# State-space parameters made in the first projection, the scan spread between the steps of a sparse attention written out over all heads

## What is computed

```python
proj = h @ w_in                       # h: normed x
u, q, k, v, qi, ki, wi, gates = split(proj)
# state-space branch, 32 groups of 16 channels, 64 complex states each
abar = exp(ar * dt) * (cos(ai * dt) + i sin(ai * dt))
coef = (abar - 1) / (ar + i ai)
s_t = abar * s_(t-1) + coef * (B @ u_t)
y = gelu(real(C @ s) + D_skip * u)
y = y * sigmoid(y @ w_glu + b_glu)
# sparse attention, 8 heads of 64, one shared key head: of the visible keys
# the 256 with the best index score take part
o = softmax(q k^T / 8 over the chosen keys) @ v
merged = sigmoid(g_ssm) * (y @ w_proj_ssm) + sigmoid(g_att) * (o @ w_proj_attn)
```

## Time and profile before

| | us |
|---|---|
| median of 3 runs | 4801.21 (4798.48 to 4808.43) |
| profiled execution | 4806.75 |
| its span in the profile | 4805.1 |

### The profile page before, as it was taken

The page is one execution under the profiler, slowest core; times in us unless marked ns, Lnnn a source line. Parts: engine busy times, 40 slices in busy tenths (PEclk is TensorE's granted clock), DMA queues, the critical chain, the costliest instruction groups (busy, mean ns, idle before and its releaser), DMA issues. The chain is left out here.

```text
span 4805.1 us, 54891 instructions
## 1 busy us (share of the span) xinstructions
PE 4013.4 (84%) x20836; PEld 3406.9 (71%) x20836; DVE 2033.1 (42%) x3688; ACT 1524.9 (32%) x2712; POOL 1522.1 (32%) x1187
## 2 busy tenths in 40 slices
PE   8598741568999989999999674666999999999878
PEld 6467641447888878788888553555879888988867
DVE  2289436332200013353111255875346666566623
ACT  2144531011200013321111233554334555545433
POOL 1121102013332324211111253322445555555433
PEclk9789875589999999998999776877999999999989
DMA  3122110035312144422221233332521111111044
GB/s 114 55 69 76 41 31 9 12 138 198 131 59 79 42 148 156 128 94 99 101 85 64 71 98 88 78 81 81 176 78 36 45 44 36 45 45 42 22 153 140
DMA packets 279840, 395.28 MB, mean 82 GB/s; under 512 B 56075, under 2 KB 183212, under 8 KB 279596
## 3 DMA queue, kind: packets, MB, share of 16 engines
q1 hardware_dynamic: 249452, 290.08, 20.0%
q0 software_dynamic: 27856, 97.88, 5.4%
q10 hardware_dynamic: 2304, 4.20, 0.2%
HBM read 285.72 MB, written 101.01 MB: 80 GB/s over the span
## 5 line engine op out<-in xcount | busy, mean ns | idle before, releaser
L112 PE MATMUL out_acc<-out_sw,out_sa 128*128 128x512 f32 x1920 | 447.0, 396 | 50.3 <-POOL out_sa L606 43.0
L112 PEld LDWEIGHTS out_acc<-out_sw,out_sa 128*128 128x128 f32 x1920 | 367.0, 191 | 130.3 <-issue 44.3
L112 PE MATMUL hg_acc<-l_XT,hg_ws 128*128 128x512 f32 x1440 | 360.3, 408 | 0.0
L112 PE MATMUL hg_acc<-l_first_ws,l_XT 128*128 128x256 f32 x2880 | 359.6, 284 | 0.0
L112 PEld LDWEIGHTS hg_acc<-l_first_ws,l_XT 128*128 128x128 f32 x2880 | 348.8, 192 | 0.0
L112 PEld LDWEIGHTS hg_acc<-l_XT,hg_ws 128*128 128x128 f32 x1440 | 278.5, 197 | 57.8
L3238 POOL TENSOR_TENSOR hg_DD<-hg_BB 128x256 f32<-128x256 f32 x224 | 157.1, 701 | 355.3 <-PE hg_pA L3002 228.8
L112 PE MATMUL up_acc<-ffn_XT,ffn_first_ws 128*128 128x512 f32 x1152 | 263.6, 391 | 2.7 <-PEq L52 2.7
L112 PE MATMUL down_acc<-down_sw,down_sa 128*128 128x512 f32 x1056 | 241.9, 391 | 19.1 <-POOL down_sa L606 16.7
L606 POOL TENSOR_TENSOR out_sa<-out_a,out_sa 128x512 fp32r<-128x512 f32 x80 | 175.8, 2198 | 253.1 <-ACT out_sw L505 253.0
L112 PEld LDWEIGHTS up_acc<-ffn_XT,ffn_first_ws 128*128 128x128 f32 x1152 | 217.3, 189 | 48.0 <-issue 2.9
(11 more groups left out here) (489 smaller groups left out, 8219.3 us busy)
## 6 DMA issues: line engine op xcount, KB each, us to landing
l_first_raw<-in_odd_w_in SPq DMA_DIRECT2D x62, 512.0 KB, 5.4
down_w<-in_w_ffn_down SPq DMA_DIRECT2D x44, 512.0 KB, 3.8
da_raw<-q_k SPq DMA_DIRECT2D x32, 512.0 KB, 8.3
out_w<-in_even_w_out SPq DMA_DIRECT2D x32, 512.0 KB, 4.3
out_w<-in_odd_w_out SPq DMA_DIRECT2D x32, 512.0 KB, 4.3
even_w<-in_even_w_in SPq DMA_DIRECT2D x7, 2048.0 KB, 9.2
l_first_raw<-in_even_w_in SPq DMA_DIRECT2D x6, 2048.0 KB, 9.1
hidden<-up_h POOLq DMA_DIRECT2D x44, 256.0 KB, 2.3
```

Of the source, the lines that this page charges most:

```text
L112: mm = pe.matmul(out, lhs(p, k), rhs(q, k), start=start and i == 0, stop=stop and i == n - 1)
```

## The change

**Parameters.** A new class `StateSpace` holds the parameters' buffers. Its eight loads are issued by SP at the end of `input_norm`, behind the first weights. `first_projection` takes the place of `project`: its weights have one raw buffer in place of two, SP in place of POOL issues the stores, DVE does the parameters between the splits, POOL makes `Wn`, and behind the last product TensorE transposes `Wn` and makes the kernels through the same banks, evictions and stage buffers. E, CP, the transposed input weights and the kernels go to memory (`kept`).

**Attention and scan.** `attend_and_scan` takes the place of `sparse_attend` and `s5_branch`. It has no loop: all 64 items are written out and numbered through, and the queries of the next pair are rounded at the middle of a pair. Logits have three buffers instead of four; `pO` is one bank instead of two, and the bank set free is `acc`, the only one of the scan branch. The table `place` says at which item and spot each of 40 groups of four (transposed inputs, input sums, output sums, transposed outputs, mixing) stands. The scan is cut in two halves of 1024 elements and 32 steps, one behind each item from 11 on. `CP` takes the buffer of E, and `MT` that of the input weights, when the scan has ended.

The diff, cut to its core:

```diff
 # input_norm, SP
                 pre.load(sp, pre_ld)
+                ss.load(sp)
 # first_projection, SP
+                load(1)
+                for i in range(N + TURNS + KERNELS):
+                    b = i % B
+                    sp.wait_ge(moved, i + 1)
...
+                    if i == G - 2:
+                        sp.wait_ge(e_made, 1)
+                        sp.dma_start(kept["E"], ss.wide[:, 0:S_E]).then_inc(e_st, DMA)
+                        sp.dma_start(kept["m8"], at["m8"]).then_inc(e_st, DMA)
+                    if i % G == G - 1 and i // G + 2 < len(chunks):
+                        load(i // G + 2)
+                    if i == N - 1:
+                        sp.wait_ge(cp_made, 1)
+                        sp.dma_start(kept["CP"], ss.wide[:, :]).then_inc(cp_st, DMA)
 # DVE
+                dve.wait_ge(ss.loaded, ss.loads * DMA)
+                expm1_of("e", "ldt", 5)
...
+                dve.wait_ge(phase, 2)
...
+                dve.sem_inc(e_made, 1)
+                split_weights(1)
...
+                dve.sem_inc(powers, 1)
+                dve.wait_ge(e_st, 2 * DMA)
+                for k in range(S_T + 1):
+                    if k == 1:
+                        split_weights(2)
+                    ss.cmul(dve, link, (CP[:, 0, :, k, :], CP[:, 1, :, k, :]), (ss.Cn[:, 0, :, :], ss.Cn[:, 1, :, :]),
+                            [wide_of(q) for q in pw(k)], shape, neg=True)
 # ACT, behind the eviction of group 1
+                    if i == 1:
+                        act.wait_ge(phase_in, 1)
+                        act.activation(at["sn"], at["r"], ACT.Sin).then_inc(phase, 1)
+                        act.activation(at["cs"], at["h"], ACT.Sin).then_inc(phase, 1)
 # attend_and_scan
+    for k in range(8):
+        place[2 + k // 2, k % 2] = TURN_U + k
+        place[6 + k // 2, k % 2] = SUM_IN + k
+        place[44 + k, 1] = SUM_OUT + k
+        place[53 + k // 2, k % 2] = TURN_Y + k
+        place[57 + k // 2, k % 2] = MIX + k
+    SCAN_AT, GELU_AT, SIGMOID_AT, MULT_AT = 11, 52, 61, 61
 # SP
+                sp.wait_ge(scanned, 1)
+                sp.dma_start(s_wide[:, :], kept["CP"]).then_inc(cp_ld, DMA)
+                sp.wait_ge(zeroed, 1)
+                for s in range(S_T):
+                    sp.dma_start(MT[s * S_CH:(s + 1) * S_CH, :, s * S_CH:P], kept["K"][:, :, 0:P - s * S_CH]).then_inc(mt_ld, DMA)
 # POOL
+                for h in range(PAIRS):
+                    if h + 1 < PAIRS:
+                        lower_queries(h + 1)
...
+                    if h == 2:
+                        pool.wait_ge(scanned, 1)
+                        pool.memset(MT, 0.0).then_inc(zeroed, 1)
 # PE
+                def sum_outputs(k):
+                    if k == 0:
+                        pe.wait_ge(in_moved, 8)
+                        pe.wait_ge(scanned, 1)
+                        pe.wait_ge(cp_ld, DMA)
+                        pe.wait_ge(mt_ld, S_T * DMA)
+                    else:
+                        pe.wait_ge(out_add, k)
...
+                for n in range(ITEMS + 2):
+                    if n + 2 < ITEMS:
+                        logits(n + 2)
+                    scan_part(n, 0)
+                    if n >= 2:
+                        values(n - 2)
+                    if n < ITEMS:
+                        turn(n)
+                    if n % 2 == 0 and n >= 4:
+                        turn_output((n - 4) // 2)
+                    scan_part(n, 1)
 # DVE
+                for n in range(ITEMS + 2):
+                    if n + 1 < ITEMS:
+                        mask(n + 1)
+                    if n % 2 and n >= 5:
+                        move_output((n - 5) // 2)
+                    if n >= 2:
+                        norm(n - 2)
+                    scan_part(n, 0)
+                    scan_part(n, 1)
+                    if n >= SCAN_AT:
+                        next(steps, None)
+                    if MULT_AT <= n < MULT_AT + 4:
+                        gate_output(2 * (n - MULT_AT))
+                        gate_output(2 * (n - MULT_AT) + 1)
 # ACT
+                for n in range(ITEMS):
+                    if n + 1 < ITEMS:
+                        exps(n + 1)
+                    scan_part(n, 0)
+                    move(n)
+                    scan_part(n, 1)
+                    if n == 0:
+                        regroup()
+                    if n % N == N // 2 and n // N + 1 < PAIRS:
+                        upper_queries(n // N + 1)
+                    if n == GELU_AT:
+                        act.wait_ge(out_add, 8)
+                        for s in range(S_T):
+                            act.activation(uc[:, s, :], uc[:, s, :], ACT.Gelu_apprx_tanh).then_inc(gelu, 1)
+                    if n == SIGMOID_AT:
+                        for i in range(8):
+                            act.wait_ge(mix_moved, i + 1)
+                            act.activation(mix[:, i, :], mix[:, i, :], ACT.Sigmoid).then_inc(gate, 1)
```

More of the change, by code:

```diff
@@ new lines, in sum_inputs @@
+                def sum_inputs(k):
+                    if k == 0:
+                        pe.wait_ge(u_moved, 8)
+                        pe.wait_ge(wt_ld, DMA)
+                    else:
+                        pe.wait_ge(in_moved, k)
+                    for q in range(4):
+                        j = 4 * (k % 4) + q
+                        for a in range(2):
+                            rows = slice(a * S_N, (a + 1) * S_N)
+                            mm = pe.matmul(acc[rows, q, :], WT[:, k // 4, j, rows], U[:, 2 * j + a, :],
+                                           start=True, stop=True, skip_group_check=True)
+                    mm.then_inc(in_sum, 1)
@@ new lines, in _ @@
+                pe.wait_ge(k_split, 1)
+                logits(0)
+                logits(1)
+                for n in range(ITEMS + 2):
[9 more added lines that the diff above has]
+                    scan_part(n, 1)
```

1143 lines of the change are left out of this document (562 added, 581 removed).

## The result

| | before | after |
|---|---|---|
| median of the runs, us | 4799.84 (4 runs, 4798.02 to 4808.43) | 4724.27 (4 runs, 4720.10 to 4740.60) |
| profiled execution, us | 4806.75 | 4725.88 |
| its span, us | 4805.1 | 4724.2 |

The account below looks back on a forecast made before the run. A chain, not an engine's capacity, was taken as the bound. Parameters in the first projection +33.5 us, attention with scan -219.1: 4806.75 - 185.6 = 4621.2, median 5.5 lower, so 4616 us; range 4560 to 4690 (8 in 10).

Parts of the forecast that it names:

- output sums: Attention and scan stage: eight groups of matmuls taking 30 to 60 us depending on the clock; 45 taken.
- The stop: Before the first output sum: TensorE waits for CP and the shifted kernels, 18 us, ends 12 and 22.
- The port: Scan steps on DVE: one each blocked by POOL's product and three query subtractions; 8 us, ends 0 and 16.
- The mixing: Late in the attention and scan stage: mixing matmuls with nothing to hide them, 28 us.
- my terms of 137 and 26: New stage: 137 us for attention over all heads; 26 for scan steps that narrow items don't hide, including 3 for clock.
- rival 3: New stage: engines take turns in a ring, stage 536 us, whole 4836; sign: narrow items over 4 us, DVE not busy; chance 0.03.
- ACT's blocks: GELU in item 52 and sigmoid in item 61, whole on ACT with four table loads: 7 + 6 us.
- the tail of the first projection: Behind the last product: 16 more groups, evictions and stores; 19 us more, ends 8 and 22.
- 1: Rival: the low clock stays from the stop to the end; +91 us, 4706 us; chance 0.08.
- 4: Rival: the whole attention and scan stage at clock 0.50; +149 us, 4764 us; chance 0.03.
- 2: Rival: pieces hide better, DVE steps and port cost nothing, output sums near full clock; 4570 us and below; chance 0.10.
- 5: Rival: first projection doesn't hide the parameters; 15 to 20 us more, 4633 us; inside the forecast's 0.76.

Follow-up runs that it names:

- attention_alone: The changed kernel with the scan branch left out of the attention stage (zeros stored in its place); 4499.8 us.
- old_order: two_banks with the order of the kernel before on TensorE and DVE (output turned ahead of the exponentials, copied right behind the normalization); 4475.15 us.
- two_banks: attention_alone with values and turned outputs in two PSUM banks in place of one; 4497.78 us.
- move_first: The changed kernel with another DVE order in an item: copy of the turned output, mask, scan step, normalization; 4696.21 us.
- full_rows: The changed kernel with the output sums' CP matmuls contracting all 128 rows in place of 64, giving other sums; 4699.04 us.
- masked_rows: The changed kernel with output sums contracting all 128 rows and right results, POOL copying states beside rows of zeros; 4692.69 us.
- copies_only: The changed kernel with GELU and sigmoid replaced by plain copies on ACT; 4724.45 us.
- steps_two_banks: two_banks with the scan recurrence's 36 DVE operations put back in items 11 to 43, on zeros; 4545.03 us.

## Why the prediction was right and wrong

**Right.** The parameters are hidden: start of the stage +5.6 (I had 5), second chunk +12.6 (11.5), end of the products +14.9 (14.5). The stop was there, 722.26 to 738.13, with 14.5 us of idle for 18 (the sign that I gave for it was 16 to 20). The port blocked one step, 6.64 in place of 1.22, so 5.4 (8). The mixing took 40.2 us for items 57 to 60, with their attention 39 by my terms. The inputs cost 18.6 (items 0 to 10 take 40.1 us, in attention_alone 21.5) against 16. The 8.93 us gaps at the seams are gone.

**Where the stage's 73 us lie.** By stretches, against my terms, with old_order's item starts as the attention's share (in the last row with the end of the stage, my 4):

| items | measured | terms | over | of it the order |
|---|---|---|---|---|
| 0 to 10 | 40.1 | 18.9 + 16 | 5 | 3 |
| 11 to 43 | 138.5 | 72.0 + 26 + 8 | 32 | 31 |
| 44 to 51 | 95.5 | 17.2 + 18 + 45 | 15 | 2 |
| 52 to the merge | 97.2 | 35.7 + 46 | 16 | 4 |

The last column is two_banks less old_order, item by item, and in the second row also what the steps cost more there (52.1 - 29.9). The rows add up to 68; the other 4.5 are old_order's own, which took 145.5 us from the first logits to the merge where I had 137 + 4.

**Wrong, the step on attention and scan (40 us in the reduced kernels, 24 of them shown in the whole one).** I wrote "TensorE is late next, and stays it" and took the pace of the kernel before, 32.9 us a pair. That pace belongs to an order: the turned output ahead of the exponentials on TensorE, and its copy right behind the normalization on DVE. In that order a pair took 34.5 us (old_order), in the order of the change 38.9 (two_banks), and so my terms of 137 and 26 came out as 159.0 and 52.4. The diff moves the copy to the next item, behind the next mask, and so behind the scan step as well, while TensorE's next values wait for it. I priced what the change adds to each queue and did not compare the order of what was there already. Giving the old order back to 30 items of the whole kernel returned 24 us. My rival 3 ("the engines take turns") named the ring and said "acc, pE and pO are one buffer each", which was the wrong culprit, and it priced the stage at 536 us, where it took 388. The ring is there, at a fraction of that. The sign that I had given for it, narrow items of over 4 us with DVE not busy, was there in part: the fifteen items from 607.3 to 667.9 us took 4.0 us in the mean with DVE busy 42.08 of 60.60 us, but of the narrow ones among them only items 16 and 20 took over 4 (6.1 and 6.3), and the longest, 9.1, is a wide one. How much of the order's price is TensorE's move and how much DVE's was not taken apart; move_first, which changes the order on DVE alone, gained 16.5 us in items 11 to 43.

**Wrong, a mis-sized term: output sums (13 us).** I took 45, halfway between 30 and 60, because "beside them is attention, whose work did raise it". Less the attention's 19.2 (attention_alone) and the stop's 14.5, the sums took 61.8. full_rows and masked_rows show that it goes with the 64-row form: with it these items took 95.5 us and 108.2 in another execution, with all 128 rows 65, which leaves 32 for the sums. The row stood in my own groups: 60 us of such work at 0.50 (1.2 GHz), TensorE busy all the time. That was the nearest row, and I argued it away. The Trainium skill (TensorE: Matmul & The Clock Gate, Why this matters for your kernels) says that a matmul over few rows takes the time of one over all of them. For one instruction at one clock the rows agree (272 and 275 ns at the least), but the mean clock granted over these items differed between the forms (0.64 and 0.82), and with it the time.

**Wrong, terms left small: ACT's blocks (12 us in items 52 to 63) and the tail of the first projection (12 us).** The copies of the transposed outputs took 1.1 us where I had 0.60, and each of ACT's two blocks 6.8 us with little of it beside TensorE. copies_only took 5.5 of the 12 out; the rest is read from the timeline, and no run shows it. In the tail, 21.35 us of matmuls had no price (11.2 in the kernel before, where the clock was 1.00), and 7.5 us lay behind CP's store. With all 128 rows the next stage's first transfer came 5.3 us earlier, and moving that store returned 5.6.

**Open: 20 us in stages that are not edited.** Before the attention it is 6 us. In the masks and gates the granted clock was 0.95 where it had been 0.99:

```profile
420.00:517.00 97.00, 88.24 (x370) 71.42 (x368) 93.65 (x217) 41.04 (x74) 16.37 (x5) 0.95 0.21 71
```

That row does not explain them: steps_two_banks has 0.95 in the same place, and its stretch from the first transfer to the first logits took 313.0 us, where the kernel before took 314.0 and the changed kernel 319.9. In the twelve other kernels with the same first stages it took 313.0 to 320.0, which makes it -1 to +6 with nothing edited; what it goes with is not shown. The 14 behind the merge are not so plain. From the first product of the merge to the last product of the output stage it is 3759.6 us before and 3773.4 after:

```profile
L112 PE MATMUL merge_acc<-merge_y,merge_w x384: 387/389/796, 936.7 to 1033.1; 128*128 128x512 f32 x192
...
L112 PE MATMUL out_acc<-out_sw,out_sa x1920: 387/389/767, 1048.2 to 4710.1; 128*128 128x512 f32 x192
```

In the other kernels this same stretch took 3754.9 to 3758.3 where the scan branch, its TensorE part or its steps were left out, and 3761.2 to 3773.6 where all of it was there. Nothing in it is edited in any of them. The traces tell where half of it lies. In the differential attention of the second model DVE stands idle twice, 3.61 and 3.46 us, in front of a mask, and the profile shows nothing that it waits for (`<-issue`):

```profile
2997.12 0.42 DVE L2727 CUSTOM_DVE_ANT_0 da_S<-da_pS,da_B 128x256 f32<-128x256 f32 x1 [3.61 <-issue]
```

All ten kernels with the whole scan branch have these two (3.0 to 3.8 us each), and the kernel before and the six others have none. From its first logits to the next output projection that stage took 396.0 us before, 405.1 after, 398.3 to 406.1 in the ten, and 393.9 to 395.1 in the six. What DVE waits for there, and where the other 5 us are, no run tells.

Of the rivals, 1 did not happen (mixing ran at 1.00), nor did 4 (items 0 to 10 were granted 0.88) or 2, and 5 covers the tail in part (31 us for 19, where it had 22).

## What to carry to other kernels

When a loop is written out anew, put the two orders of each queue side by side, the lines that stay too. Here two moved lines, a transposition on TensorE and a copy of 0.29 us on DVE, made the attention 17.2 us longer by themselves, and the 36 added DVE operations of the scan cost 52.1 us in place of 29.9. Work put between the steps of a ring (engines that wait for each other in turn) belongs behind whatever the other engine is waiting for. And a pace or a clock taken from a row holds for the order and the form of that row alone.

## What the runs showed of the hardware

- Over the eight output sums and the attention beside them the granted clock was 0.63 with TensorE busy 76.05 of 80 us where two of three of the sums' matmuls used 64 rows, and 0.89 with 43.18 of 50 us busy where all used 128. For the 128 matmuls of the kernels in the first projection, behind an idle of 7.5 us, it was 0.50 with 64 rows and 0.89 with 128; the same with 64 rows, behind transposes without an idle, was granted 1.00 for its 11.2 us in the kernel before.
- A PSUM bank more or less cost nothing measurable by itself (4497.78 against 4499.8 us).
- An ACT copy from PSUM of 128 x 512 into places that are eight elements apart took 1.11 us, and 0.60 into neighbouring ones; DVE took 1.08 for the copies of transposed outputs before.
- A DVE operation with two SBUF inputs that met a POOL operation of 8.91 us lasted until 1.1 us after it (6.64 in place of 1.22), as one of 2.28 us that met a product of 8.87 ended 2.1 us after it in the earlier trace rows.
